# Value tiles of their own in a dilated attention branch, and one tile in place of two for the low halves of the queries

## Chip, cores, metric

One Trainium2 chip, one of its NeuronCores. The metric is device time in microseconds of one execution of the whole program, lower is better. Before the change it is 3742.44 us (median of three runs, 3741.66 to 3744.21).

## What is computed

Two blocks of two layers each, one after the other, over 1024 tokens of width 1024. The change touches the first block only. Each of its layers has three branches on the same normed input; the first and the third are attention:

```python
proj = jnp.einsum('bsd,dc->bsc', h, w_in)
aq, ak, av, az, buv, bz, cq, ck, cv, cz, gl = split_cols(proj)
# first branch: 4 heads, two maps of 64 dims each, causal
qa = partial_rope(aq...); ka = partial_rope(ak...)
oa = diff_attention(qa, ka, va, lam)
# third branch: 8 heads of 64 dims, three dilated windows, their softmaxes merged
qc = partial_rope(cq...); kc = partial_rope(ck...)
oc = sum over patterns of softmax(lse) * dilated_window_attention(qc, kc, vc, window, dil)
yc = oc.reshape(B, S, C_WIDTH) * jax.nn.silu(cz)
pb = jnp.einsum('nbsc,ncd->nbsd', ys, w_branch)
merged = jnp.einsum('bsnd,nbsd->bsd', jax.nn.sigmoid(gl...), pb)
```

The projections `cq`, `ck`, `cv`, `cz` and the gates `gl` all start from the same `h`, so their order is free.

## The kernel before

**Number format.** A float32 value is held as a rounded upper half in fp32r and the remainder as a lower half. A product of two such values takes three TensorE passes (upper by upper, lower by upper, upper by lower). A projection unit is 512 tokens of one block of 128 output columns: 8 contraction blocks by 3 passes, 24 matmuls of 512 columns at L1578, into one PSUM bank. A projection of one name has two such units (tokens 0 to 511, 512 to 1023) on one weight tile. GpSimd makes the two halves of each weight tile (`Whi` at L3001, `Wlo` at L3003) when the tile that stood in that place has been used for the last time; there are three places.

**Order.** Nothing schedules at run time. The class `Order` writes one list of units in Python; each engine's program walks through that list and issues its own part of every unit, in list order, with semaphore waits where a unit needs another's result. `put` and `run` append units. `u["inside"] = {k: [...]}` has TensorE issue another unit's part after contraction block k of u, while the other engines see that unit where it stands in the list.

**Third branch, `attention_c` (L890).** The loop runs over 32 steps: 4 pairs of heads (j), 2 heads (h), 4 groups of 256 queries (i, with 2i+2 key blocks). In step s TensorE issues, in this order: `turn` (transposes of the softmax weights of s at L1705, first into bank `pt`), the scores of s+1 (L1673, L1674), the projection units that the list `amid` gives to this step, and `values` (weights by values, L1721). Behind the scores run, for s+1: VectorE's masked minimum (L2631), ScalarE's exponential (L2042), VectorE's reciprocal (L2673), ScalarE's scaling (L2046). Then come the transposes, ScalarE's upper halves (L2072) and VectorE's lower halves (L2683). The projections in `amid` are what TensorE does meanwhile. Twelve units belong to a pair: two each for values v, the gate z, queries q, keys k, and four for the branch gates g, which are stored to DRAM for later. Before, they are placed so (line 974 to 978): step 0 v0 v1, step 1 z0, step 2 z1, steps 3 to 5 g0 g1 g2, step 6 q0 g3 k0, step 7 q1 k1, where q and k are those of the next pair.

**Queries and keys (`qk`).** VectorE rotates a unit: shuffle L2500, L2504, L2507, L2510, in `tmp0` and `tmp1`. ScalarE writes upper halves (L1983, L1986), VectorE lower halves (L2517 for queries, L2519 for keys). A tile holds two heads in its rows 0 to 63 and 64 to 127 (`ROWS`). `KK[h]` holds head h's keys, upper half in `ROWS[h]` and lower half in the other rows; `QQ[h]` holds the query's upper half twice. So one matmul of 128 contraction rows gives upper by upper plus upper by lower (L1673). A second one (L1674) takes the query's lower halves from `QL[h]`, whose other 64 rows are zero; the unit `clear` (L2590) zeroes them by two VectorE memsets (L2595) at the start of each of the four attention stages.

**Values.** A value unit is projected; ScalarE copies the bank to `tmp0` or `tmp1` (L1994), the same tiles that rotation uses, so the copy waits for the rotation of the units ahead of it; TensorE transposes the copy (unit `v_turn`, L1660) into `pt`; ScalarE and VectorE write halves `VP` (L2007, L2664).

The first branch has the same queries and keys, its own order of units, and 32 steps too.

Of the kernel before, what the change touches and what calls it, by code (L numbers as in the profile page):

```python
# [91 lines left out]
def memory(nc, t):  # L92
# [50 lines left out]
    m.QL = [at(f"QL{i}", o + 4096 * i, [P, S], F32R) for i in range(2)]; o += 8192  # L143
# [3 lines left out]
    m.tmp = [at(f"tmp{i}", o + 2048 * i, [P, 512]) for i in range(4)]; o += 8192  # L147
# [184 lines left out]
class Order:  # L332
# [355 lines left out]
    def attention(self, l, br):  # L688
        diff = br == "a"
        self.tmp_free = [None] * 4  # L690
# [22 lines left out]
        def v_units(j):  # L713
            buf = j % 2
            copied = {}

            def sets(u):
                u["tmp_free"] = listed(self.tmp_free[u.i])
                copied[u.i] = ("v_copied", u.id)

            def turned(u):
                u["copied"], u["rel"] = copied[u.i], v_free[buf:buf + 1] if diff else v_free[:]
                self.tmp_free[u.i] = ("v_turned", u.id)
# [4 lines left out]
            return (self.in1("value", l, COL[br + "v"] + j * P, box={}, sets=sets, emptied="v_copied")  # L728
                    + [Unit(kind="v_turn", i=i, buf=buf, banked=diff, sets=turned, diff=diff, emptied=out if diff else None)
                       for i in range(2)])  # L730
# [21 lines left out]
        cleared = ("cleared", self.put("clear").id)  # L752
# [11 lines left out]
        if not diff:  # L764
            self.banks = NARROW
            self.attention_c(l, qk, vtok, v_free, qk_units, v_units, z_units, gate_units(2), cleared, attended, ztok)
            return
# [14 lines left out]
        def scores(s):  # L782
# [3 lines left out]
                         ready=[x for y in keys for x in y] + [cleared])  # L786
# [103 lines left out]
    def attention_c(self, l, qk, vtok, v_free, qk_units, v_units, z_units, gates, cleared, attended, ztok):  # L890
# [10 lines left out]
        def scores(s, within=False):  # L901
            j, h, i = steps[s]
            keys = [qk["q"][i // 2], qk["k"][0]] + ([qk["k"][1]] if i >= 2 else [])
            scored[s] = self.put("scores", **geometry(s), within=within, ready=[x for y in keys for x in y] + [cleared],
# [54 lines left out]
        self.run([q0, k0, q1])  # L959
# [4 lines left out]
        v = v_units(0)  # L964
        for s, (j, h, i) in enumerate(steps):
            more = s + 1 < len(steps)
            if s % 8 == 0:
# [571 lines left out]
def listed(x):  # L1539
    return x if isinstance(x, list) else [x]  # L1540
# [5 lines left out]
def tensor_program(pe, m, order):  # L1546
# [107 lines left out]
    def v_turn(u):  # L1654
# [4 lines left out]
        for c in range(4):  # L1659
            x = pe.e.transpose(bank[:, c * P:c * P + P], m.tmp[u.i][:, c * P:c * P + P], ident[:, :])  # L1660
        x.then_inc(*pe.tick("v_turned", u.id))

    def scores(u):
        for i, (h, qb) in enumerate(u.maps):
# [5 lines left out]
            for c0 in range(0, nk, 512):  # L1670
# [3 lines left out]
                x = pe.e.matmul(out, m.QL[h][:, qs], m.KK[h][:, c0:c0 + n], start=False, stop=True)  # L1674
# [183 lines left out]
def scalar_program(act, m, order):  # L1858
# [130 lines left out]
    def value(u):  # L1989
# [4 lines left out]
        act.e.activation(m.tmp[u.i][:, :], m.pj[u.bank][:, 0:u.n], ACT.Copy).then_inc(*act.tick("v_copied", u.id))  # L1994
# [304 lines left out]
def vector_program(dve, m, order):  # L2299
# [192 lines left out]
    def qk(u):  # L2492
# [19 lines left out]
        for h, r in enumerate(ROWS):  # L2512
# [3 lines left out]
            if u.name == "q":  # L2516
                TT(m.QL[h][r, c], t1[r, :], m.QQ[h][r, c].bitcast(F32), ALU.subtract).then_inc(*dve.tick("qk_lo", u.id, h))  # L2517
# [454 lines left out]
    parts = {"phase": phase, "start": start, "clear": clear, "square": square, "sums": sums, "last_sums": last_sums, "norm": norm,  # L2972
# [447 lines left out]
```

## Time and profile before

| | us |
|---|---|
| median of three runs | 3742.44 |
| lowest, highest | 3741.66, 3744.21 |
| the profiled execution | 3745.62 |
| its span, from first to last instruction | 3743.6 |
| third branch, first score to last value, layer 1 and 2 | 777.5 to 1149, 2029.6 to 2401 |
| first branch, the same | 363.8 to 666, 1616.1 to 1917 |
| granted TensorE clock, mean | 0.984 |

The profiled execution is 3.18 us over the median. Engines are named PE (TensorE matmul), PEld (its weight loads), DVE (VectorE), ACT (ScalarE), POOL (GpSimd), SP (the queue that issues DMAs). A timeline row gives the start in us, the busy time, engine, line, operation, the tiles written and read, the shape, how many are merged in the row, and in brackets the idle time before it with what ended it. Matmul records overlap, since a matmul's end is its pipeline's end: the pitch of a stream is the distance of two starts.

### The profile page before, as it was taken

The numbers are of one execution on the slowest core, as the hardware profiler recorded it, in microseconds if no ns is written. First come the engines' busy times: TensorE is split into PE (matmuls) and PEld (weight loads), VectorE is DVE, ScalarE is ACT, GpSimd is POOL, SyncE is SP. The second block draws the span as 40 slices with busy tenths as digits, with TensorE's granted clock in tenths as the row PEclk, the third lists the DMA queues.
The fourth block names the chain that finished last, engine by engine and source line by source line (L and its number), as shares of the span: only waits on it lengthen the run. The fifth ranks groups of instructions, "written<-read, shape, count | busy, mean of one in ns | idle before, by whom it ended". The sixth has DMA issues, their size and how long they took to land.

```text
span 3743.6 us, 49479 instructions
## 1 busy us (share of the span) xinstructions
PE 3581.0 (96%) x19870; PEld 3173.4 (85%) x19870; DVE 1873.8 (50%) x3550; ACT 1356.2 (36%) x2965; POOL 1089.9 (29%) x794
## 2 busy tenths in 40 slices
PE   6999999999999999999999999999999999999998
PEld 5888887778887788888877888878999999999998
DVE  5444555356666553155534666655334546424543
ACT  3212444045553121044422555423235532225541
POOL 3632322322222254322322222233530013641111
PEclk9999999999999999999999999999999999999999
DMA  3122111411114311211123111341210012211012
GB/s 108 44 75 71 34 40 40 141 56 46 43 46 157 116 57 51 85 34 40 46 91 105 42 46 46 111 160 48 66 51 21 29 63 89 70 54 33 27 43 91
DMA packets 85476, 244.80 MB, mean 65 GB/s; under 512 B 10752, under 2 KB 24832, under 8 KB 85248
## 3 DMA queue, kind: packets, MB, share of 16 engines
q1 hardware_dynamic: 85248, 241.66, 19.6%
q8 instruction: 156, 2.56, 0.3%
q14 instruction: 72, 0.59, 0.1%
HBM read 191.09 MB, written 50.53 MB: 65 GB/s over the span
## 4 chain that ended last, share of the span: by engine, by line
PE 75%; DVE 12%; ACT 5%; issue 3%; POOL 2%; DMA 1%; SPq 0%; DVEq 0%; POOLq 0%; ACTq 0%
PE pj L1578 28%; PE pS L1578 27%; PE po L1829 4%; PE pS L1809 3%; PE pS L1811 2%; PE po L1721 1%; PE pS L1673 1%; PE pS L1674 1%; DVE tmp L2507 1%; DVE KK L2519 1%; DVE tmp L2510 1%; PE po L1695 1%; PE pj L1821 1%; ACT P L2035 1%; DVE tmp L2500 1%
## 5 line engine op out<-in xcount | busy, mean ns | idle before, releaser
L3001 POOL TENSOR_SCALAR Whi<-stage 128x1024 fp32r<-128x1024 f32 (+3 forms) x252 | 259.5, 1030 | 1833.2 <-PE pj L1578 981.0
L1578 PE MATMUL pj<-Hhi,Whi 128*128 128x512 f32 x1616 | 646.5, 400 | 0.7 <-DVE tmp L2504 0.7
L1578 PE MATMUL pj<-Hhi,Wlo 128*128 128x512 f32 x1616 | 634.7, 393 | 0.0
L1578 PE MATMUL pj<-Hlo,Whi 128*128 128x512 f32 x1616 | 633.0, 392 | 0.0
L3003 POOL TENSOR_TENSOR Wlo<-stage,Whi 128x1024 fp32r<-128x1024 f32 (+3 forms) x252 | 598.5, 2375 | 21.0
L1578 PEld LDWEIGHTS pj<-Hhi,Wlo 128*128 128x128 f32 x1616 | 305.4, 189 | 66.0
L1578 PEld LDWEIGHTS pj<-Hhi,Whi 128*128 128x128 f32 x1616 | 306.6, 190 | 63.9 <-DVE tmp L2504 2.1
L1578 PE MATMUL pS<-Hhi,Whi 128*128 128x512 f32 x816 | 328.1, 402 | 29.4 <-DVE Hlo L2372 13.5
L1578 PEld LDWEIGHTS pj<-Hlo,Whi 128*128 128x128 f32 x1616 | 306.2, 189 | 59.0
L1578 PE MATMUL pS<-Hlo,Whi 128*128 128x512 f32 x816 | 325.0, 398 | 0.0
L1578 PE MATMUL pS<-Hhi,Wlo 128*128 128x512 f32 x816 | 324.4, 398 | 0.0
L1578 PEld LDWEIGHTS pS<-Hhi,Whi 128*128 128x128 f32 x816 | 158.1, 194 | 65.4 <-DVE Hlo L2372 15.2
L2631 DVE CUSTOM_DVE_ANT_0 P<-pS,mask 128x128 f32<-128x128 f32 (+7 forms) x256 | 185.7, 752 | 26.7 <-PE pj L1685 12.0
L1578 PE MATMUL pS<-H2hi,Whi 128*128 128x348 f32 (+1 forms) x576 | 186.8, 324 | 5.1 <-DVE H2lo L2372 3.6
L1578 PEld LDWEIGHTS pS<-Hhi,Wlo 128*128 128x128 f32 x816 | 157.6, 193 | 34.1
L1578 PE MATMUL pS<-H2lo,Whi 128*128 128x348 f32 (+1 forms) x576 | 186.0, 323 | 0.0
L1578 PE MATMUL pS<-H2hi,Wlo 128*128 128x348 f32 (+1 forms) x576 | 185.7, 322 | 0.0
L1578 PEld LDWEIGHTS pS<-Hlo,Whi 128*128 128x128 f32 x816 | 157.7, 193 | 32.6
L2926 DVE TENSOR_REDUCE st<-pS 116x1 f32<-116x1044 f32 (+2 forms) x68 | 84.7, 1245 | 152.1 <-PE pS L1811 151.7
L3049 POOL TENSOR_TENSOR st<-st,vec 128x1 f32<-128x1 f32 x64 | 35.2, 551 | 429.1 <-DVE st L2652 429.1
L1673 PE MATMUL pS<-KK,QQ 128*128 128x512 f32 (+3 forms) x384 | 140.5, 374 | 10.4 <-DVE KK L2519 9.0
L1883 ACT ACTIVATE sq<-X 128x512 f32<-128x512 f32 (+2 forms) x84 | 47.2, 562 | 269.4 <-DVE X L2809 134.7
(485 smaller groups left out, 8013.4 us busy)
## 6 DMA issues: line engine op xcount, KB each, us to landing
stage<-wstream SPq DMA_DIRECT2D x228, 512.0 KB, 3.6
merged<-Mb SPq DMA_DIRECT2D x32, 512.0 KB, 2.8
Mb<-merged SPq DMA_DIRECT2D x32, 512.0 KB, 5.2
gates<-tmp SPq DMA_DIRECT2D x48, 256.0 KB, 2.2
TH<-gates SPq DMA_DIRECT2D x24, 512.0 KB, 6.0
xres<-X SPq DMA_DIRECT2D x16, 520.0 KB, 2.9
xr<-xres SPq DMA_DIRECT2D x16, 520.0 KB, 4.1
X<-xT SPq DMA_DIRECT2D x16, 256.0 KB, 7.1
```

Source lines behind the costliest of these rows:

```text
L1578: x = pe.e.matmul(ps, w[a][:, v.koff + k * P:v.koff + k * P + P], moving(v.of, b, k, v.t0, v.n), start=k == 0 and i == 0, stop=k == v.K - ...
L1673: pe.e.matmul(out, m.QQ[h][:, qs], m.KK[h][:, c0:c0 + n], start=True, stop=False)
L1674: x = pe.e.matmul(out, m.QL[h][:, qs], m.KK[h][:, c0:c0 + n], start=False, stop=True)
L1695: x = pe.e.matmul(m.po[:, 0:P], m.PT[u.pt][:, kb, :], m.V[u.j % 2][:, kb, :], start=kb == 0, stop=kb == u.nb - 1)
L1809: pe.e.matmul(out, q[a][:, qs], m.kn[b][:, t], start=i == 0, stop=False)
L1811: x = pe.e.matmul(out, r[a][:, qs], m.KR[:, t], start=False, stop=a == 1)
L1829: x = pe.e.matmul(m.po[0:u.nq, 0:P], m.PT2[u.l][0:n, i, 0:u.nq], m.V2[u.h][i // 7][0:n, i % 7, :], start=i == 0, stop=i == 8)
L1883: act.e.activation(dst, src, ACT.Square).then_inc(*act.tick("square", u.id))
L2631: dve.e.tensor_tensor_reduce(m.Pm[u.p[i]][:, 0:qb * P + P], m.pS[:, 1024 * i:1024 * i + qb * P + P], m.mask[:, 896 - P * qb:1024], 1.0, 3e ...
L2926: dve.e.tensor_reduce(st[0:u.nq, u.col:u.col + 1], m.pS[0:u.nq, 0:1536].rearrange("p (c n) -> p c n", c=3)[:, :, 0:348], AX.XY, ALU.min).t ...
L3001: pool.e.tensor_scalar(upper, stage, 1.0, 0.0, ALU.mult, ALU.add).then_inc(*pool.tick("whi", c))
L3003: TT(lower, stage, upper.bitcast(F32), ALU.subtract).then_inc(*pool.tick("wlo", c))
```

## The change

1. `QL` is one tile of 128 rows: rows 0 to 63 hold the lower halves of the first head, 64 to 127 those of the second. The second score matmul uses `QL[ROWS[h]]` and `KK[h][ROWS[h]]`, 64 contraction rows. The unit `clear` and every wait for it are gone.
2. In the place of the second `QL` tile stand two tiles `vt0`, `vt1`. In the third branch values are copied there and turned from there; in the first branch they stay in `tmp0`, `tmp1`.
3. In the third branch the values of the next pair are projected in steps 4 and 5, q0 g2 k0 in step 6, q1 g3 k1 in step 7; z0 and z1 in steps 0 and 1, g0 and g1 in 2 and 3. The transposes of the values stand inside z0 and z1, after contraction block 1. In the last pair, which has no next one, steps 4 and 7 have no projection (before: step 7 alone). At the branch's start the order is q0 v0 k0 v1 q1 k1 in place of q0 k0 q1 k1 and then, in step 0, v0 v1.

```diff
-    m.QL = [at(f"QL{i}", o + 4096 * i, [P, S], F32R) for i in range(2)]; o += 8192
+    m.QL = at("QL", o, [P, S], F32R); o += 4096
+    own = [at(f"vt{i}", o + 2048 * i, [P, 512]) for i in range(2)]; o += 4096
...
-    m.tmp = [at(f"tmp{i}", o + 2048 * i, [P, 512]) for i in range(4)]; o += 8192
+    m.tmp = [at(f"tmp{i}", o + 2048 * i, [P, 512]) for i in range(4)] + own; o += 8192
...
         def v_units(j):
-            buf = j % 2
+            buf, t = j % 2, 0 if diff else 4
...
-                u["tmp_free"] = listed(self.tmp_free[u.i])
+                u["tmp_free"] = listed(self.tmp_free[t + u.i])
...
-        cleared = ("cleared", self.put("clear").id)
...
-        self.run([q0, k0, q1])
+        v = v_units(0)
+        self.run([q0, v[0], k0, v[1], q1])
         k1["inside"] = {4: [scores(0, True)]}
...
-                v[1]["inside"], z[0]["inside"] = {5: v[2:3]}, {3: v[3:4]}
-                amid = [v[0:1] + v[2:3] + v[1:2], v[3:4] + z[0:1], z[1:2], g[0:1], g[1:2], g[2:3], g[3:4], []]
+                z[0]["inside"], z[1]["inside"] = {1: v[2:3]}, {1: v[3:4]}
+                amid = [v[2:3] + z[0:1], v[3:4] + z[1:2], g[0:1], g[1:2], [], g[2:3], g[3:4], []]
                 if j < 3:
                     read, v = [], v_units(j + 1)
                     q, k = qk_units(j + 1, {(x, i): read for x in "qk" for i in range(2)})
-                    amid[6], amid[7] = [q[0], g[3], k[0]], k[1:2]
+                    amid[4:] = [v[0:1], v[1:2], [q[0], g[2], k[0]], [g[3], k[1]]]
...
-            x = pe.e.transpose(bank[:, c * P:c * P + P], m.tmp[u.i][:, c * P:c * P + P], ident[:, :])
+            x = pe.e.transpose(bank[:, c * P:c * P + P], m.tmp[u.t + u.i][:, c * P:c * P + P], ident[:, :])
...
-                x = pe.e.matmul(out, m.QL[h][:, qs], m.KK[h][:, c0:c0 + n], start=False, stop=True)
+                x = pe.e.matmul(out, m.QL[ROWS[h], qs], m.KK[h][ROWS[h], c0:c0 + n], start=False, stop=True)
...
-                TT(m.QL[h][r, c], t1[r, :], m.QQ[h][r, c].bitcast(F32), ALU.subtract).then_inc(*dve.tick("qk_lo", u.id, h))
+                TT(m.QL[r, c], t1[r, :], m.QQ[h][r, c].bitcast(F32), ALU.subtract).then_inc(*dve.tick("qk_lo", u.id, h))
...
-    def clear(u):
-
-        for x in u.ph:
-            dve.wait_ge(x)
-        for h in range(2):
-            dve.e.memset(m.QL[h][ROWS[1 - h], :].bitcast(F32), 0.0).then_inc(*dve.tick("cleared", u.id, h))
-        dve.mark("cleared", u.id)
```

What moves is seen best on ScalarE where one pair gives way to the next (`PC` weights turned, `P` weights, `VP` values turned; L2072 upper halves of the turned weights). Before:

```order
L1983 ACTIVATE KK_84<-tmp_93 64x512
L1983 ACTIVATE KK_85<-tmp_93 64x512
L2072 ACTIVATE PC_101<-pt 128x128
L2072 ACTIVATE PC_101<-pt 128x2x128
L2081 ACTIVATE tmp_95<-po 64x256
...
L1870 ACTIVATE Yhi<-tmp_95 64x512
L1994 ACTIVATE tmp_92<-pj 128x512
L2007 ACTIVATE VP_90<-pt 128x4x64
L2007 ACTIVATE VP_91<-pt 128x4x64
L1994 ACTIVATE tmp_93<-pj 128x512
```

and now:

```order
L1959 ACTIVATE tmp_95<-pj 128x512
L1983 ACTIVATE KK_84<-tmp_94 64x512
L1983 ACTIVATE KK_85<-tmp_94 64x512
L2072 ACTIVATE PC_102<-pt 128x128
L2072 ACTIVATE PC_102<-pt 128x2x128
L2081 ACTIVATE tmp_96<-po 64x256
...
L1870 ACTIVATE Yhi<-tmp_96 64x512
L2007 ACTIVATE VP_91<-pt 128x4x64
L2007 ACTIVATE VP_92<-pt 128x4x64
L1965 ACTIVATE tmp_95<-pj 128x512
```

The copies of the value units (L1994) have left this place for steps 4 and 5 of the pair before, and a gate (L1959) stands ahead of the last key unit.

On TensorE the fifth step of the last pair (first layer), which reads before, up to its first two projection matmuls:

```order
L1705 MATMUL pt<-ident,P_96 128x128
L1705 MATMUL pt<-ident,P_97 128x128 x2
L1673 MATMUL pS<-KK_85,QQ_83 128x384
L1674 MATMUL pS<-KK_85,QL_87 128x384
L1673 MATMUL pS<-KK_85,QQ_83 128x512
L1674 MATMUL pS<-KK_85,QL_87 128x512
L1578 MATMUL pj<-Hhi,Whi_62 128x512
L1578 MATMUL pj<-Hlo,Whi_62 128x512
```

now reads, into the sixth:

```order
L1705 MATMUL pt<-ident,P_97 128x128
L1705 MATMUL pt<-ident,P_98 128x128 x2
L1673 MATMUL pS<-KK_85,QQ_83 128x384
L1674 MATMUL pS<-KK_85,QL 128x384
L1673 MATMUL pS<-KK_85,QQ_83 128x512
L1674 MATMUL pS<-KK_85,QL 128x512
L1721 MATMUL po<-PC_102,VP_92 128x256
L1721 MATMUL po<-PC_104,VP_92 128x256
L1721 MATMUL po<-PC_102,VP_92 128x128
L1721 MATMUL po<-PC_104,VP_92 128x128
L1705 MATMUL pt<-ident,P_97 128x128 x3
L1705 MATMUL pj<-ident,P_98 128x128 x4
```

The 24 projection matmuls between the scores and the values of this step are gone. The order of the score matmuls, one of `QQ` and one of `QL` in turn, is as it was.

## Rows read from the trace of the kernel before

**Rows 1.** The page: busy time, and engines in the chain that ended last

```profile
PE 3581.0 (96%) x19870; PEld 3173.4 (85%) x19870; DVE 1873.8 (50%) x3550; ACT 1356.2 (36%) x2965; POOL 1089.9 (29%) x794
...
PE 75%; DVE 12%; ACT 5%; issue 3%; POOL 2%; DMA 1%; SPq 0%; DVEq 0%; POOLq 0%; ACTq 0%
```

**Rows 2.** PE waits over the whole span: us in total, times, longest

```profile
PE pt L1660 <- ACT tmp L1994: 15.8, 6, 2.6
...
PE pt L1705 <- ACT P L2046: 9.6, 2, 6.2
PE pS L1673 <- DVE KK L2519: 9.0, 8, 2.0
```

**Rows 3.** Groups of tile QL: duration ns min/median/max, first and last start

```profile
L1674 PE MATMUL pS<-KK,QL x384: 272/387/628, 364.0 to 2388.2; 128*128 128x512 f32 x136, 128*128 128x128 f32 x24, 128*128 128x384 f32 x24, 128*128 128x256 f32 x8
...
L2595 DVE MEMSET QL<- x8: 912/912/912, 333.8 to 2016.1; 64x1024 f32 x8
```

**Rows 4.** PE timeline round a 16-row matmul: start us, us busy, instruction, [idle before]

```profile
2542.91 0.40 PE L1578 MATMUL pj<-Hlo,Whi 128*128 128x512 f32 x1
2543.14 0.39 PE L1578 MATMUL pj<-Hhi,Wlo 128*128 128x512 f32 x1
2543.46 1.25 PE L1614 MATMUL pS<-ident,st 16*128 16x16 f32 x8
2544.47 0.48 PE L1578 MATMUL pj<-Hhi,Whi 128*128 128x512 f32 x1
```

**Rows 5.** PE timeline, the same line L1614 with 128 rows throughout

```profile
2563.17 1.05 PE L1614 MATMUL pj<-ident,st 128*128 128x128 f32 x8
2564.05 0.39 PE L1614 MATMUL pS<-ident,st 128*128 128x128 f32 x2
2564.20 0.40 PE L1578 MATMUL pS<-H2hi,Whi 128*128 128x348 f32 x1
```

**Rows 6.** Timeline of PE where pair 0 of heads gives way to pair 1

```profile
879.42 0.40 PE L1578 MATMUL pj<-Hhi,Wlo 128*128 128x512 f32 x1
...
882.67 0.39 PE L1578 MATMUL pj<-Hhi,Whi 128*128 128x512 f32 x1
...
891.96 0.39 PE L1578 MATMUL pj<-Hhi,Wlo 128*128 128x512 f32 x1
894.98 0.65 PE L1660 MATMUL pt<-ident,tmp 128*128 128x128 f32 x4 [2.63 <-ACT tmp L1994]
...
897.26 0.65 PE L1721 MATMUL po<-PC,VP 128*128 128x256 f32 x4 [0.24 <-DVE VP L2664]
```

**Rows 7.** Timeline of DVE, the same stretch

```profile
875.99 2.63 DVE L2507 TENSOR_TENSOR tmp<-tmp,sin 128x512 f32<-128x512 f32 x1
...
884.41 0.74 DVE L2500 STREAM_SHUFFLE tmp<-pj 128x512 f32<-128x512 f32 x1
...
887.96 1.40 DVE L2519 TENSOR_TENSOR KK<-tmp,KK 64x512 fp32r<-64x512 f32 x2 [0.70 <-ACT KK L1983]
889.39 0.62 DVE L2683 TENSOR_TENSOR PC<-pt,PC 128x128 fp32r<-128x128 f32 x2
```

**Rows 8.** Timeline of POOL, the same stretch

```profile
875.67 2.39 POOL L3003 TENSOR_TENSOR Wlo<-stage,Whi 128x1024 fp32r<-128x1024 f32 x1
```

**Rows 9.** Timeline of ACT, the same stretch

```profile
892.44 1.21 ACT L2046 ACTIVATE P<-P,st 128x384 f32<-128x384 f32 x2
...
895.67 0.66 ACT L2007 ACTIVATE VP<-pt 128x256 fp32r<-128x256 f32 x2 [0.74 <-PE pt L1660]
```

**Rows 10.** PE timeline, first transposes of a fifth step (here of the last pair)

```profile
1117.33 0.51 PE L1705 MATMUL pt<-ident,P 128*128 128x128 f32 x3
```

**Rows 11.** ACT timeline, the weights of the step after it

```profile
1121.25 1.22 ACT L2046 ACTIVATE P<-P,st 128x384 f32<-128x384 f32 x2
```

**Rows 12.** Timeline of PE at the start of the third branch, first layer

```profile
786.46 1.14 PE L1705 MATMUL pt<-ident,P 128*128 128x128 f32 x3 [6.19 <-ACT P L2046]
```

**Rows 13.** Timeline of DVE where the first branch starts its softmax

```profile
364.29 0.29 DVE L2631 CUSTOM_DVE_ANT_0 P<-pS,mask 128x128 f32<-128x128 f32 x1 [3.01 <-PE pS L1674]
```

More of the change, by code:

```diff
@@ L689, in attention @@
         diff = br == "a"
-        self.tmp_free = [None] * 4
+        self.tmp_free = [None] * 6
         qk = {"q": [None] * 2, "k": [None] * 2}
@@ L722, in turned @@
                 u["copied"], u["rel"] = copied[u.i], v_free[buf:buf + 1] if diff else v_free[:]
-                self.tmp_free[u.i] = ("v_turned", u.id)
+                self.tmp_free[t + u.i] = ("v_turned", u.id)
                 vtok[buf][u.i] = (out, u.id)
@@ L727, in v_units @@
             out = "v_out" if diff else "v_low"
-            return (self.in1("value", l, COL[br + "v"] + j * P, box={}, sets=sets, emptied="v_copied")
-                    + [Unit(kind="v_turn", i=i, buf=buf, banked=diff, sets=turned, diff=diff, emptied=out if diff else None)
+            return (self.in1("value", l, COL[br + "v"] + j * P, box={}, sets=sets, t=t, emptied="v_copied")
+                    + [Unit(kind="v_turn", i=i, t=t, buf=buf, banked=diff, sets=turned, diff=diff, emptied=out if diff else None)
                        for i in range(2)])
@@ L765, in attention @@
             self.banks = NARROW
-            self.attention_c(l, qk, vtok, v_free, qk_units, v_units, z_units, gate_units(2), cleared, attended, ztok)
+            self.attention_c(l, qk, vtok, v_free, qk_units, v_units, z_units, gate_units(2), attended, ztok)
             return
@@ L785, in scores @@
             u = self.put("scores", **geometry(s), free=[("masked", softened[s - 1].id, m) if s else None for m in (0, 0, 1, 1)],
-                         ready=[x for y in keys for x in y] + [cleared])
+                         ready=[x for y in keys for x in y])
             scored[s] = u
@@ L888, in attention, with attention_c @@
         attended(softened[s], scored[s])
-    def attention_c(self, l, qk, vtok, v_free, qk_units, v_units, z_units, gates, cleared, attended, ztok):
+    def attention_c(self, l, qk, vtok, v_free, qk_units, v_units, z_units, gates, attended, ztok):
         steps = [(j, h, i) for j in range(4) for h in range(2) for i in range(4)]
@@ L903, in scores @@
             keys = [qk["q"][i // 2], qk["k"][0]] + ([qk["k"][1]] if i >= 2 else [])
-            scored[s] = self.put("scores", **geometry(s), within=within, ready=[x for y in keys for x in y] + [cleared],
+            scored[s] = self.put("scores", **geometry(s), within=within, ready=[x for y in keys for x in y],
                                  free=[("masked", softened[s - 1].id, m) if s else None for m in (0, 0, 1, 1)])
@@ L963, in attention_c @@
         self.run([k1])
-        v = v_units(0)
         for s, (j, h, i) in enumerate(steps):
@@ L1993, in value @@
         phase_met(u)
-        act.e.activation(m.tmp[u.i][:, :], m.pj[u.bank][:, 0:u.n], ACT.Copy).then_inc(*act.tick("v_copied", u.id))
+        act.e.activation(m.tmp[u.t + u.i][:, :], m.pj[u.bank][:, 0:u.n], ACT.Copy).then_inc(*act.tick("v_copied", u.id))
     def v_turn(u):
@@ L2970, in last @@
                 op1=ALU.mult).then_inc(*dve.tick("final2", u.c, k))
-    parts = {"phase": phase, "start": start, "clear": clear, "square": square, "sums": sums, "last_sums": last_sums, "norm": norm,
+    parts = {"phase": phase, "start": start, "square": square, "sums": sums, "last_sums": last_sums, "norm": norm,
              "table": table, "proj": proj,
```

## The prediction

> **What bounds the kernel.** I read the page first: which engine is busy, and which one the chain that ended last runs along. TensorE is busy for 96% of the span and makes 75% of the chain [rows 1]. So a wait is worth what it holds TensorE up, and an instruction of another engine is worth nothing by itself. Then I read what TensorE waits for [rows 2]. In the third branch three causes stand out: six waits for the copy of the values (15.8 us), two for the first softmax weights (9.6 us), eight for key halves (9.0 us, some 4 of them at the two starts of this branch, by the timeline). The change aims at these. Last I read what else it touches in TensorE's stream: 384 matmuls of `QL`, each between two others of 128 rows [rows 3]. They become matmuls of 64 rows. A faster or slower form of them lies on the path in full. A difference of 0.2%, 7.5 us, is about what a measurement of this kernel tells from none.
>
> **1. The 64-row matmuls.** No row shows a 64-row matmul. The trace has one place where a matmul uses fewer row groups of the array than its neighbours: L1614 with 16 rows, after and before matmuls of 128. An ordinary pitch of 512 columns is 2543.14 - 2542.91 = 0.23 us; to the 16-row matmul it is 0.32 [rows 4]. In the control, the same line with 128 rows, eight starts take 2564.05 - 2563.17 = 0.88 us, 0.11 each, and the last two take 0.15 up to the next fp32r matmul, 0.07 less than 0.22 [rows 5]. So from 2543.14 to the first L1578 behind it, one pitch of 0.23 and eight of 0.11 less 0.07, 1.04 us, would be expected; it took 2544.47 - 2543.14 = 1.33 [rows 4]. One way into the narrow form and one way out cost 0.29 us, though the narrow matmuls stream 16 columns and not 128. I take 0.29 us for each of the 384, since this is the nearest row by far: 111 us. Bounds: below, nothing (64 rows may be treated otherwise than 16; a gain is excluded, as the columns streamed stay the same and no two 64-row matmuls are neighbours). Above, each matmul waits for the whole of the one before (0.39 us) and for a weight load of 0.19 that is no longer hidden, in place of a 0.23 pitch: 0.35 for each of 768 changes, 269 us. None of this is covered: scores lie between transposes and projections of a busy engine.
>
> The Trainium skill, page "TensorE: Matmul & The Clock Gate", section "Why this matters for your kernels", states that a single small-K matmul takes the same time as one with K=128. By it the 111 us would be zero; that is a rival below. The page "TensorEngine Tiling (Array Packing)", section "Tiling Modes", says that a change of the tiling mode drains the engine, without a figure; the 0.29 us agree.
>
> **2. Where one pair gives way to the next, six times.** Now the transposes of the values wait 894.98 - 891.96 - 0.23 = 2.8 us for the copy, and the first values 0.4 us more for `VP` [rows 6]: 3.2 us. After the change the copy is made long before, and the transposes stand 6 matmuls into z0. What is late next is bank `pt`: VectorE has to take the lower halves of the turned weights from it (L2683), and that is queued behind the last key unit. Count from the last projection matmul of k1 (879.42). TensorE needs 882.67 - 879.42 = 3.25 us to the next projection [rows 6], 0.6 more for two pairs of scores by term 1, and 6 pitches of 0.23: it arrives at 5.2. VectorE starts k1's rotation at 0.5 (the gate now ahead of k1 lets it be idle by then) and needs 887.96 + 1.40 - 884.41 = 4.95 when nothing disturbs it [rows 7]. But the weight split follows each last use of a weight tile, and while POOL's L3003 runs [rows 8] VectorE's L2507 takes 2.63 us in place of 0.68 [rows 7], 1.95 more. I assume the same for k1, whose end frees a weight tile. So its keys are ready at 7.4, and `pt` at 7.4 + 0.65 (889.36 to 890.01) = 8.05: a wait of 2.85. Then 4 transposes, 0.5, and 18 matmuls, 4.1, bring TensorE to values at 12.7. `VP` needs the softmax chain of the next step, which ends 893.65 - 889.36 = 4.3 after the keys [rows 7, 9], a conversion of Y, which I put at 0.65, and from `VP`'s start to the values 897.26 - 895.67 = 1.6 [rows 6, 9]: 7.4 + 6.55 = 13.95, a wait of 1.25. Together 4.1 against 3.2: +0.9, six times, **+5 us**. The wait doesn't go, it changes its cause. Bounds: -19 if both waits vanish; +20 if VectorE's unit ends as late as now (9.9 after the matmul, 2.5 more).
>
> **3. The last pair.** Its fifth step loses its cover. From its transposes, 1117.33 [rows 10], to the first weights of the step after, 1121.25 + 0.61 [rows 11], are 4.5 us. TensorE has 0.3 of transposes, 0.9 + 0.6 of scores and 0.45 of values to do. That leaves 2.3, and 0.3 more for the second map's weights: 2.6 us in each layer, **+5**. Bounds 0 to +8.
>
> **4. The branch's start.** Now the first transposes wait 6.2 us in layer 1 [rows 12], 3.4 in layer 2 (9.6 in all [rows 2]), and scores about 2 each time. Behind the change the scores stand 11 us of values later than k0 and don't wait, but the last two units, q1 and k1, still follow each other, and the softmax is queued on VectorE behind q1 with a weight split beside it. With term 2's times for a rotation I get some 3.8 us for the weights and 2.3 for `pt`, 6.1 against 9.7 and 6.8 with the small gaps: **-4** for both. Bounds -13 to 0.
>
> **5. The memsets.** Eight of 0.91 us [rows 3], on VectorE. In the first branch the softmax starts after an idle time of 3.0 us of VectorE, in wait for scores [rows 13]: nothing. In the third they are in term 4.
>
> **6. The rest** costs nothing: ScalarE's copies are the same number and ScalarE is 36% busy; POOL splits as many tiles; SP's gate DMAs only change places. If TensorE's longer steps give covers elsewhere, that is below 0.3 us a step.
>
> **Sum.** 111 + 5 + 5 - 4 = +117 us. The profiled execution took 3745.62, 3.2 over the median; so 3742.4 + 117 = **3859 us**, 3.1% slower.
>
> **Rivals.**
> - *No price for 64 rows.* For it: the narrow row in the trace is one case, of 16 rows and of another number format. Against it: the way out of the narrow form has no semaphore wait in it, and it is slow there too. Without the longer scores term 2 is 1.5 each, +9, term 3 is +6, term 4 about -2: 3742.4 + 13 = 3755 us, still slower. This is the case of the skill's small-K rule. 0.14.
> - *Faster.* 64 rows cost nothing, and the keys are ready before TensorE gets to the transposes. The point from which it decides: k1's lower halves must end within 4 us of k1's last matmul, not 7.4; it would need POOL's split to fall elsewhere and a shorter rotation. Then -19 in term 2, -4 in term 4, +5 in term 3: 3724 us. Against it stands the undisturbed 4.95. 0.05.
> - *Full exposure.* The bound above of term 1: 3742.4 + 269 + 6 = 4017 us. The odd row gives half of it. 0.04.
> - The change not doing what it says is term 2 itself: the tiles are free, another wait takes the place. It is in every case but the second.
>
> **Numbers.** The forecast has 0.77. Its own range takes term 1 between 0.15 and 0.36 us for each matmul (one way of 0.09 in and as much less out; both ways at the narrow row's worst) and the other terms' nearer bounds: 3790 to 3900. To leave out no more than 2 in 10 I reach down a little, to 3785. Slower by over 0.2%: forecast, full exposure and nine tenths of the first rival, 0.93, cut to 0.91 for what I haven't thought of. Within: 0.03. Faster: 0.06.
>
> **What would show it.** In the profile after: the start of a `QL` matmul 0.09 us or more later behind its `QQ` neighbour than the 0.23 pitch of 512 columns, weight loads of scores no longer beside the matmul before, and the scores' stretch longer by 0.29 for each pair. Six waits of L1660 now put down to VectorE's L2683 in place of ScalarE's copy, of 2 to 4 us; waits of L1721 for `VP` of about 1 us; two waits of L1705 of some 2.5 us in the last pairs. No memset L2595. I am wrong if the pitch of `QL` matmuls stays 0.23, and wrong on term 2 if L1660 has no wait in the third branch.

## The result, and the profile after

| | before | after |
|---|---|---|
| median, us | 3743.32 (4 runs, 3741.66 to 3748.87) | 3886.32 (4 runs, 3877.61 to 3896.09) |
| profiled execution, its span | 3745.62, 3743.6 | 3884.86, 3883.1 |
| granted TensorE clock, mean | 0.984 | 0.979 |
| start of the first to start of the last `QQ` score matmul, first branch, layers 1 and 2 | 288.2, 287.4 | 315.5, 311.1 |
| the same, third branch | 357.9, 358.4 | 392.9, 392.7 |

The changed kernel is slower, by a ratio of 1.038 (95% interval 1.0353 to 1.0407). The forecast was 3859, 3.1% slower, with a range of 3785 to 3900. So the direction held, and the loss was 143 us where 117 were forecast. The spans of the two profiled executions differ by 139.5 us; the accounts below are made against that.

The page of the profile after: busy time, chain, and the groups of the two score matmuls (columns: line, engine, operation, count | busy us, mean ns | idle before).

```profile
PE 3731.9 (96%) x19870; PEld 3202.5 (82%) x19870; DVE 1866.8 (48%) x3542; ACT 1357.1 (35%) x2965; POOL 1089.5 (28%) x794
...
PE 86%; DVE 6%; ACT 2%; issue 2%; DMA 1%; POOL 1%; SPq 0%; DVEq 0%; POOLq 0%; ACTq 0%
...
L1674 PE MATMUL pS<-KK,QL 64*128 64x512 f32 (+3 forms) x384 | 171.5, 447 | 0.0
L1673 PE MATMUL pS<-KK,QQ 128*128 128x512 f32 (+3 forms) x384 | 169.7, 442 | 0.9 <-ACT V L2004 0.9
```

TensorE made 75% of the chain before [rows 1] and makes 86% now. It has the same 19870 instructions and is busy for 3731.9 us where it was for 3581.0: the same work got longer. The median `QL` matmul lasts 491 ns where it lasted 387 [rows 3], and its `QQ` neighbour 474 where it lasted 390.

What TensorE waits for, after (us in total, times, longest):

```profile
PE pt L1660 <- DVE PC L2675: 19.0, 6, 3.3
PE pt L1705 <- ACT P L2046: 13.4, 4, 5.0
...
PE pt L1728 <- ACT PT L2054: 7.3, 13, 0.8
PE pt L1685 <- DVE st L2644: 5.9, 2, 2.9
...
PE po L1721 <- DVE VP L2656: 2.2, 2, 1.1
```

Against [rows 2]: the copy of the values has gone as a cause, and the same six transposes wait longer, for bank `pt`. The waits for key halves (9.0 us) are gone. L1728, the transposes of the first branch's results, waited 15.2 us before, in 19 places.

**The scores.** I call a matmul of 128 rows wide and one of 64 rows narrow, and each step from one to the other, either way, a change of form. TensorE after, where wide and narrow matmuls of 512 columns stand in turn, and its weight loads there:

```profile
503.86 0.48 PE L1673 MATMUL pS<-KK,QQ 128*128 128x512 f32 x1
504.27 0.49 PE L1674 MATMUL pS<-KK,QL 64*128 64x512 f32 x1
504.69 0.50 PE L1673 MATMUL pS<-KK,QQ 128*128 128x512 f32 x1
505.12 0.49 PE L1674 MATMUL pS<-KK,QL 64*128 64x512 f32 x1
505.54 0.50 PE L1673 MATMUL pS<-KK,QQ 128*128 128x512 f32 x1
```

```profile
504.27 0.18 PEld L1674 LDWEIGHTS pS<-KK,QL 64*128 64x128 f32 x1 [0.24 <-issue]
504.69 0.19 PEld L1673 LDWEIGHTS pS<-KK,QQ 128*128 128x128 f32 x1 [0.24 <-issue]
```

The pitch is 0.41 to 0.43 us, where 512 columns took 0.23 from a `QL` matmul to the next. In the kernel before, at such a place, TensorE's matmuls and then its weight loads:

```profile
470.70 0.39 PE L1674 MATMUL pS<-KK,QL 128*128 128x512 f32 x1
470.93 0.22 PE L1673 MATMUL pS<-KK,QQ 128*128 128x128 f32 x1
```

```profile
470.47 0.19 PEld L1674 LDWEIGHTS pS<-KK,QL 128*128 128x128 f32 x1
470.70 0.19 PEld L1673 LDWEIGHTS pS<-KK,QQ 128*128 128x128 f32 x1
```

Before, a weight load starts one matmul early (the load at 470.47 is for the matmul at 470.70) and is hidden by it. After, it starts with its own matmul (504.27 and 504.27), in both directions, and its 0.18 to 0.19 us lie bare. The medians of the pitches say the same at other widths. From a `QL` matmul to what follows: 0.23 to 0.43 us at 512 columns, 0.18 to 0.37 at 384, 0.12 to 0.31 at 256, 0.11 to 0.25 at 128: some 0.19, whatever the columns, 0.14 for the narrowest. From `QQ` to `QL` it is 0.28 to 0.43 us at 512 columns, 0.15 more, and 0.19 more at the other widths. I weight the shift of each median with its count (of `QQ` to `QL` and of `QL` to the next): 137 us for 384 matmuls, 0.36 each, 0.18 for each of 768 changes of form.

What follows the scores pays a little too. After, where a projection stands behind them:

```profile
906.74 0.50 PE L1578 MATMUL pj<-Hhi,Whi 128*128 128x512 f32 x1
907.07 0.40 PE L1578 MATMUL pj<-Hlo,Whi 128*128 128x512 f32 x1
907.31 0.40 PE L1578 MATMUL pj<-Hhi,Wlo 128*128 128x512 f32 x1
```

The first pitch of the projection, at full clock, is 0.34 us where the kernel before has 0.23 behind its scores. With some 60 such places that is 6 us, on top of the 137. With 128 rows in the new order (experiment 1) it is 0.23 again.

### The profile page after: what moved, and what is told of

Same layout as the page of the kernel before. It is cut to its first block, busy times and chain, and to the rows that moved or that the text cites. A ratio compares the mean times of both kernels' runs of the same rounds, so it can differ in the third digit from the quotient of the medians.

```text
span 3883.1 us, 49441 instructions
## 1 busy us (share of the span) xinstructions
PE 3731.9 (96%) x19870; PEld 3202.5 (82%) x19870; DVE 1866.8 (48%) x3542; ACT 1357.1 (35%) x2965; POOL 1089.5 (28%) x794
## 4 chain that ended last, share of the span: by engine, by line
PE 86%; DVE 6%; ACT 2%; issue 2%; DMA 1%; POOL 1%; SPq 0%; DVEq 0%; POOLq 0%; ACTq 0%
PE pj L1578 35%; PE pS L1578 27%; PE po L1829 4%; PE pS L1674 3%; PE pS L1673 3%; PE pS L1809 3%; PE pS L1811 2%; PE po L1721 2%; PE po L1695 1%; PE pj L1821 1%; PE pt L1685 1%; DMA TH<-gates 1%; PE pj L1705 1%; PE pt L1705 1%; DVE tmp L2510 1%
## 5 line engine op out<-in xcount | busy, mean ns | idle before, releaser
L1578 PE MATMUL pj<-Hhi,Whi 128*128 128x512 f32 x1616 | 658.3, 407 | 0.0
L2995 POOL TENSOR_TENSOR Wlo<-stage,Whi 128x1024 fp32r<-128x1024 f32 (+3 forms) x252 | 598.7, 2376 | 21.0
L1674 PE MATMUL pS<-KK,QL 64*128 64x512 f32 (+3 forms) x384 | 171.5, 447 | 0.0
L1673 PE MATMUL pS<-KK,QQ 128*128 128x512 f32 (+3 forms) x384 | 169.7, 442 | 0.9 <-ACT V L2004 0.9
```

The source lines that it names most:

```text
L1578: x = pe.e.matmul(ps, w[a][:, v.koff + k * P:v.koff + k * P + P], moving(v.of, b, k, v.t0, v.n), start=k == 0 and i == 0, stop=k == v.K - ...
L1673: pe.e.matmul(out, m.QQ[h][:, qs], m.KK[h][:, c0:c0 + n], start=True, stop=False)
L1674: x = pe.e.matmul(out, m.QL[ROWS[h], qs], m.KK[h][ROWS[h], c0:c0 + n], start=False, stop=True)
L2995: TT(lower, stage, upper.bitcast(F32), ALU.subtract).then_inc(*pool.tick("wlo", c))
```

## The experiments

**1 and 2: the narrow form and the rest of the change apart.** The first takes the changed kernel and gives the second score matmul its 128 rows back. The second puts only the 64-row matmul into the kernel before.

```diff
-                x = pe.e.matmul(out, m.QL[ROWS[h], qs], m.KK[h][ROWS[h], c0:c0 + n], start=False, stop=True)
+                x = pe.e.matmul(out, m.QL[:, qs], m.KK[h][:, c0:c0 + n], start=False, stop=True)
```

> The changed kernel with one edit: the second score matmul takes all 128 rows of QL and KK again. With one QL tile the other 64 rows now add the other head's lower halves times this head's lower key halves, a product of two remainders, of the size of those that the scheme drops anyway. So the new order, the value tiles and the missing memsets stay, the 64-row form goes. Forecast's theory (the 64-row form is nearly all of the loss): back near the kernel before, 3742 + 13 = 3755 us by the sum's terms without term 1; by the waits in the profile after (pt +3, VP +1, first weights +4, keys -9) only 3742 to 3748. Rival, the new order and its waits cost the most and the form little: 3800 us or more. Pitch of QL matmuls of 512 columns: 0.23 to 0.28 us by the first, 0.43 by the second.

Measured: 3760.27 us, ratio 1.0042 (1.0029 to 1.0055), 14.6 us above the kernel before. The forecast's theory holds: nearly all of the loss has gone with the narrow form. What is left is nearer its sum (+13) than the 3742 to 3748 that the waits in the profile after would give, because without the longer scores these waits are longer, L1660's 21.3 us in place of 19.0, and L1728 has its own back. Score matmuls stand in turn here as they do in the kernel after, on the same tiles and into the same banks, so neither the turns nor the banks make the price.

```diff
-                x = pe.e.matmul(out, m.QL[h][:, qs], m.KK[h][:, c0:c0 + n], start=False, stop=True)
+                x = pe.e.matmul(out, m.QL[h][ROWS[h], qs], m.KK[h][ROWS[h], c0:c0 + n], start=False, stop=True)
```

> The kernel before with one edit: the second score matmul takes 64 rows (both QL tiles, the memsets and the old order stay). Forecast's theory: 384 of them at 0.29 us, 3742 + 111 = 3853 us. Theory from the profile after, 768 changes of form at 0.195 us, 150 us, less 8 to 10 of waits that the longer scores cover: 3880 to 3885. Rival, the order costs the most: below 3800.

Measured: 3843.44 us, ratio 1.0274 (1.0253 to 1.0296): +98 us, less than either theory said. The pitches are those of the kernel after to 2 ns (430, 427), so the price of 137 us is the same. The rest was given back, as the waits of this kernel show:

```profile
PE pt L1728 <- ACT PT L2054: 7.2, 13, 0.8
...
PE pS L1673 <- DVE KK L2519: 3.9, 2, 1.9
...
PE pt L1705 <- ACT P L2046: 2.2, 2, 1.1
```

L1660's 15.8 us of [rows 2] have no row any more, L1705 has 2.2 of 9.6, L1673 3.9 of 9.0, L1728 7.2 of 15.2. 137 - 15.8 - 7.4 - 5.1 - 8.0 = 101. So TensorE's longer scores covered 36 us of waits in the old order. With the 6 us behind the scores the sum is 107, against 98 measured (95 between the spans): the account is good to 10 us. In the new order this cover is much smaller: 3886.32 - 3760.27 = 126 us is what the narrow form costs there.

**3 and 4: price by matmul or by change of form.** The same 384 narrow matmuls, regrouped. In 3 the `QQ` matmuls of a map come first, then its `QL` ones (512 changes of form). In 4 this is done over both maps of a unit (256 changes).

```diff
-            for c0 in range(0, nk, 512):
-                n = min(512, nk - c0)
+            tiles = [(c0, min(512, nk - c0)) for c0 in range(0, nk, 512)]
+            for c0, n in tiles:
                 out = m.pS[:, 1024 * i + c0:1024 * i + c0 + n]
                 pe.e.matmul(out, m.QQ[h][:, qs], m.KK[h][:, c0:c0 + n], start=True, stop=False)
+            for c0, n in tiles:
+                out = m.pS[:, 1024 * i + c0:1024 * i + c0 + n]
                 x = pe.e.matmul(out, m.QL[ROWS[h], qs], m.KK[h][ROWS[h], c0:c0 + n], start=False, stop=True)
```

> The changed kernel with the score matmuls of a map regrouped: first the QQ matmuls of its one or two banks, then the QL ones. The same 384 matmuls of 64 rows, but 512 changes of form in place of 768. If each change costs 0.195 us: 3886 - 50 = 3836 us. If each 64-row matmul costs 0.35 us by itself, whatever stands beside it: 3886. If the cost is the switch of the accumulating bank or the reuse of loaded weights, something else: no move, or a gain at maps of one bank too (it leaves those as they are).

> The changed kernel with the score matmuls of a whole unit regrouped: QQ matmuls of both maps, then the QL ones of both: 256 changes of form. If each change costs 0.195 us: 3886 - 100 = 3786 us, less some us given back where the second map's bank comes free late; in the first branch the 64-row matmuls of the two maps stand in different row groups and may even overlap, a few us more. If each 64-row matmul costs by itself: 3886 or above.

Measured: 3834.48 us (ratio 1.0238, 1.0224 to 1.0252) and 3784.59 us (1.0109, 1.0094 to 1.0124): 52 and 102 us below the changed kernel, where 50 and 100 were expected by change of form and none by matmul. From the start of the first to the start of the last `QQ` score matmul, mean of both layers:

| changes of form in one branch | 0 (experiment 1) | 64 (4) | 128 (3) | 192 (after) |
|---|---|---|---|---|
| third branch, us | 357.7 | 371.4 | 381.2 | 392.8 |
| first branch, us | 289.3 | 290.1 | 301.9 | 313.3 |

In the third branch this is nearly a straight line, 35.1 / 192 = 0.18 us for each change. In the first branch the steps from 64 to 128 and to 192 are as steep (11.8 and 11.4 us), and the one from 0 to 64 is 0.8 us. There the narrow matmuls of the two maps read different rows. TensorE of experiment 4, in the first branch and then in the third (rows of L1676 are the four `QL` matmuls of a unit):

```profile
487.22 1.05 PE L1672 MATMUL pS<-KK,QQ 128*128 128x512 f32 x4
488.21 0.69 PE L1676 MATMUL pS<-KK,QL 64*128 64x512 f32 x4
488.82 0.66 PE L1688 MATMUL pt<-ident,P 128*128 128x128 f32 x4
...
1119.05 1.12 PE L1672 MATMUL pS<-KK,QQ 128*128 128x512 f32 x4
1120.10 1.14 PE L1676 MATMUL pS<-KK,QL 64*128 64x512 f32 x4
1121.17 0.50 PE L1578 MATMUL pj<-Hhi,Whi 128*128 128x512 f32 x1
```

Four of 512 columns take 488.82 - 488.21 = 0.61 us in the first branch and 1121.17 - 1120.10 = 1.07 in the third, where both maps belong to one head. In the first branch the two heads' matmuls start 2 to 12 ns apart: rows 0 to 63 and 64 to 127 work side by side. What that saves (0.46 us for four of 512 columns) about pays for the two changes of form (0.36), and no more.

**5: the value tiles without the new order.** Everything of the changed kernel but its order, with 128-row matmuls.

```diff
-        v = v_units(0)
-        self.run([q0, v[0], k0, v[1], q1])
+        self.run([q0, k0, q1])
...
-                amid = [v[2:3] + z[0:1], v[3:4] + z[1:2], g[0:1], g[1:2], [], g[2:3], g[3:4], []]
+                amid = [v[0:1] + v[2:3] + v[1:2], v[3:4] + z[0:1], z[1:2], g[0:1], g[1:2], g[2:3], g[3:4], []]
...
-                    amid[4:] = [v[0:1], v[1:2], [q[0], g[2], k[0]], [g[3], k[1]]]
+                    amid[6], amid[7] = [q[0], g[3], k[0]], k[1:2]
```

> The order of the kernel before, with everything else of the changed kernel: value tiles of their own, one QL tile, no memsets, and the second score matmul on 128 rows. It tells what the tiles are worth without the new order. If the copy of the values really waits for tmp0 and tmp1, its six waits (15.8 us) and a little at the start go: 3745 - 12 = 3733 us or less. Rival, from ScalarE's timeline of the kernel before: there the copy L1994 starts at 894.33, right behind the scaling L2046 and the copy L1870 that end at 894.31, so it waits in ScalarE's queue and the tile was free since 887.3: no change, 3741 to 3748 us, and L1660 still waits 2.6 us.

Measured: 3744.16 us, ratio 0.9999 (0.9991 to 1.0008), no change. ScalarE of this kernel, and the transposes that wait for it, at one place and in all:

```profile
888.79 0.63 ACT L1870 ACTIVATE Yhi<-tmp 64x512 fp32r<-64x512 f32 x1
889.45 0.60 ACT L1994 ACTIVATE vt<-pj 128x512 f32<-128x512 f32 x1
```

```profile
890.10 0.66 PE L1660 MATMUL pt<-ident,vt 128*128 128x128 f32 x4 [2.63 <-ACT vt L1994]
```

```profile
PE pt L1660 <- ACT vt L1994: 15.8, 6, 2.6
```

The copy now has a tile of its own and still starts right behind L1870, 2.63 us late as before [rows 6], and the six waits sum to the same 15.8 us [rows 2]. It waited in ScalarE's queue, behind the softmax, and not for the tile. The memsets are gone here too and moved nothing.

**6: what makes `pt` late.** The boundary of two pairs in the kernel after, first TensorE, then VectorE, then POOL:

```profile
919.58 0.40 PE L1578 MATMUL pj<-Hhi,Wlo 128*128 128x512 f32 x1
...
924.76 0.40 PE L1578 MATMUL pj<-Hhi,Wlo 128*128 128x512 f32 x1
928.24 0.66 PE L1660 MATMUL pt<-ident,vt 128*128 128x128 f32 x4 [3.09 <-DVE PC L2675]
...
932.64 0.39 PE L1578 MATMUL pj<-Hhi,Wlo 128*128 128x512 f32 x1
934.13 0.65 PE L1721 MATMUL po<-PC,VP 128*128 128x256 f32 x4 [1.11 <-DVE VP L2656]
```

```profile
921.43 1.21 DVE L2507 TENSOR_TENSOR tmp<-tmp,sin 128x512 f32<-128x512 f32 x1
922.75 2.69 DVE L2510 SCALAR_TENSOR_TENSOR tmp<-tmp,tmp 128x512 f32<-128x512 f32 x1
926.13 1.40 DVE L2519 TENSOR_TENSOR KK<-tmp,KK 64x512 fp32r<-64x512 f32 x2 [0.69 <-ACT KK L1983]
927.57 0.62 DVE L2675 TENSOR_TENSOR PC<-pt,PC 128x128 fp32r<-128x128 f32 x2
```

```profile
922.19 2.70 POOL L2995 TENSOR_TENSOR Wlo<-stage,Whi 128x1024 fp32r<-128x1024 f32 x1
```

The whole of k1's rotation stands in VectorE's queue ahead of the lower halves that free `pt`. Counted by pitches the two waits of TensorE are 3.25 and 1.26 us, 4.5 together, each some 0.15 over its bracket. The next kernel takes experiment 1, moves k1 into the first step of the next pair, behind that pair's first softmax, and starts the branch otherwise.

```diff
-        self.run([q0, v[0], k0, v[1], q1])
-        k1["inside"] = {4: [scores(0, True)]}
+        self.run([q0, v[0], k0, v[1]])
+        q1["inside"] = {1: [scores(0, True)]}
...
-        self.run([k1])
+        self.run([q1])
+        late = k1
...
-                z[0]["inside"], z[1]["inside"] = {1: v[2:3]}, {1: v[3:4]}
-                amid = [v[2:3] + z[0:1], v[3:4] + z[1:2], g[0:1], g[1:2], [], g[2:3], g[3:4], []]
+                late["inside"], z[1]["inside"] = {1: v[2:3]}, {1: v[3:4]}
+                amid = [v[2:3] + [late], v[3:4] + z[1:2], g[0:1], g[1:2], [], g[2:3], g[3:4], []]
...
-                    amid[4:] = [v[0:1], v[1:2], [q[0], g[2], k[0]], [g[3], k[1]]]
+                    amid[4:] = [v[0:1], v[1:2], [q[0], g[2], k[0]], [g[3]]]
+                    late = k[1]
...
+                self.run(z[0:1] if s % 8 == 1 else [])
                 scores(s + 1)
```

> e1 (new order, 128 rows) with the last key unit k1 moved out of the pair's last step into the first step of the next pair, in the place of z0, and z0 in front of the second step's scores, z1 behind them. The branch starts with q0 v0 k0 v1, then the first scores inside q1, and k1 in step 0. Theory: the 4.5 us that TensorE loses where pairs change (transposes behind bank pt 3.3, values behind VP 1.1) come from k1's rotation of 5 us, which stands in VectorE's queue ahead of the lower halves of the turned weights and of the next softmax. Behind them it holds nothing up, since scores need these keys only in the step after: 3760 - 6 x 4.5 - 2 x 5 at the starts = 3723 us, and less half clock, 3715 to 3730. Rival: the rotation now holds up the weights of the second step, and the scores behind z0 wait for the keys: the waits come back there, 3745 to 3765.

Measured: 3745.03 us, ratio 1.0003 (0.9995 to 1.0012), 15 us below experiment 1 where 37 were expected. TensorE at the start of the branch, and at the first change of pairs:

```profile
789.50 1.11 PE L1663 MATMUL pt<-ident,vt 128*128 128x128 f32 x4 [7.10 <-DVE PC L2678]
...
886.26 0.66 PE L1663 MATMUL pt<-ident,vt 128*128 128x128 f32 x4 [0.89 <-DVE PC L2678]
...
892.15 0.65 PE L1724 MATMUL po<-PC,VP 128*128 128x256 f32 x4 [1.14 <-DVE VP L2659]
```

Where pairs change the theory holds in direction: by pitches 2.3 us in place of 4.5. They don't go, since now q1's rotation stands there, and it takes 9.7 us (875.9 to 885.6), with POOL splitting weights beside it twice. At the start a wait of 7.1 us has come up, behind the same q1.

**7: `pt` alone.** Experiment 1 with the transposes in a projection bank (`banked=True`).

> e1 with the transposes of the third branch's values in a projection bank, not in pt. If the 3.3 us of L1660 in wait for pt are a cause by themselves: 3760 - 20 = 3740 us. If pt is only the first of several things that k1's rotation makes late, the wait moves to the values (VP, whose copies stand in ScalarE's queue behind the next scaling): L1660 has none, L1721 waits 3 to 4.5 us at each of the six places, time 3755 to 3760.

Measured: 3768.74 us, ratio 1.0077 (1.0064 to 1.0091). The waits of this kernel:

```profile
PE po L1719 <- DVE VP L2654: 31.6, 8, 5.5
```

The transposes (L1660 above) wait no more, and the values wait, by pitches, 4.9 to 5.7 us at each of six places. In experiment 1 the two waits together were 3.6 to 4.8. This is the second theory, but 9 us above its 3755 to 3760. The bank was a link in the chain, not its cause.

**8 to 11: following the chain.** 9 is experiment 6 with the start in the order q0 k0 v0 q1 v1, the first transposes of the values inside q1. 8 has them there too, in the old start order, and moves the later ones; 10 is 9 with q1 also put behind the change of pairs; 11 is 10 with another bank for half of the second step's turned weights. Experiment 9 against experiment 6:

```diff
-        self.run([q0, v[0], k0, v[1]])
-        q1["inside"] = {1: [scores(0, True)]}
+        self.run([q0, k0, v[0]])
+        v[2]["within"] = True
+        q1["inside"] = {1: [scores(0, True)], 3: v[2:3]}
...
-        self.run([q1])
+        self.run([v[2], q1, v[1]])
...
-                late["inside"], z[1]["inside"] = {1: v[2:3]}, {1: v[3:4]}
-                amid = [v[2:3] + [late], v[3:4] + z[1:2], g[0:1], g[1:2], [], g[2:3], g[3:4], []]
+                late["inside"], z[1]["inside"] = {1: v[2:3]} if j else None, {1: v[3:4]}
+                amid = [(v[2:3] if j else []) + [late], v[3:4] + z[1:2], g[0:1], g[1:2], [], g[2:3], g[3:4], []]
```

> e6 with the first transposes of the values moved. At the branch's start they stand in q1 after contraction block 3, ahead of the first softmax weights' turn, since pt is free there; in e6 they waited 7.1 us for pt in each layer, behind q1's rotation. At the six places where pairs change they stand after block 3 of k1 in place of block 1, and ScalarE and VectorE take VP ahead of the output copy (L1873) of the pair before. Theory, from the waits of e6: 14.2 us at the two starts go, and of 2.3 us at the six places 0.65 each: 3745 - 14 - 4 = 3727 us, half clock behind the long waits a few us less. Rival: at the start VP's lower halves now hold up q1's rotation or the turn of the first weights, or the key rotations behind them wait: 3735 to 3745 us.

> e6 with another start of the third branch and nothing else: q0 k0 v0, then q1 with the first scores behind block 1 and the first transposes of the values behind block 3, then v1, then k1 in step 0. In e6 TensorE lost 7.3 us there in each layer, in wait for pt behind q1's rotation (9 us, two of its operations stretched beside POOL's splits). With v1 between q1 and the first weights the rotation has 5.5 us more: 3745 - 2 x 6 = 3733 us. Rival: the half-stretched rotation still comes out late at the first values or the second weights, 3738 to 3745.

> e9 with q1 as well behind the change of pairs: step 7 has only g3 (scores inside it), step 0 q1, step 1 k1 and z0, scores, z1. At the six places no rotation then stands ahead of the turned weights' lower halves: the wait of 1.05 us for pt goes, the one for VP (1.3) may stay or halve: e9 - 6 x 1.5 = 3724 us. Rival, as e8 showed it: with two banks a projection now starts right behind the one whose bank VectorE has not read yet, and waits 1 to 3.6 us there, six times: e9 + 5 to + 15.

> e10 with one edit: in the pair's second step the second half of the turned weights goes to the second score bank of map 0, which the short scores of this step leave free, in place of a projection bank. In e10 z0 waits 3.2 to 4.0 us there, six times, since VectorE reads that bank behind q1's rotation. If this bank was the cause: 3759 - 22 = 3737 us, and with the waits at the places where pairs change at 0.6 us in place of e9's 2.35, half clock less too, down to 3726. Rival: z1 now waits for the bank that k1's rotation reads, or the scores for the new bank: 3745 or more.

| | us | ratio (interval) | the wait that came up in TensorE |
|---|---|---|---|
| 8 | 3765.24 | 1.0051 (1.0038 to 1.0065) | z0 for the bank that k1's rotation reads, 6 times; values at each start, 3.2 us |
| 9 | 3735.72 | 0.9974 (0.9963 to 0.9985) | none of this size |
| 10 | 3759.49 | 1.0036 (1.0024 to 1.0048) | z0 for a bank behind q1's rotation, 6 times |
| 11 | 3761.79 | 1.0048 (1.0035 to 1.0062) | second step's scores for k1's keys; scores for the new bank once in each layer, 3.5 us |

Their rows in the lists of waits, of 8, 10 and 11:

```profile
PE pj L1584 <- DVE tmp L2510: 20.6, 6, 3.4
```

```profile
PE pj L1582 <- DVE PC L2679: 22.0, 6, 3.8
```

```profile
PE pS L1682 <- DVE KK L2528: 27.1, 14, 3.5
```

8, 10 and 11 are misses: 3727, 3724 and 3737 us were expected. The rivals foresaw that another wait would come up, but for 8 and 10 not how much: 3735 to 3745 and 3741 to 3751 were their ranges, 3765 and 3759 came. Each experiment removes the wait it aims at, and another of 3 to 4 us comes up. I read this as two rotations of 5 to 10 us on VectorE that must pass somewhere in this stretch; no run takes one of them away to show it. Part of the size is the clock: the traces have 139 us at half clock in 8 and 145 in 10, against 121 in 6 and 118 in 9, and in 8 the stretch 890.8 to 897.5, behind a wait of 3.4 us of z0, is one of them. Only at the start was there room. **Experiment 9 beats both kernels**, the one before by 0.26% and the one after by 151 us. Its 9 us below experiment 6 are 3 short of what was expected: scores now wait for k1's keys, up to 2.0 us, in the place of the 7.1. Its own rows:

```profile
PE pS L1677 <- DVE KK L2523: 10.1, 10, 2.0
...
PE pt L1664 <- DVE PC L2679: 5.4, 6, 0.9
```

## Why the prediction was right, and where it was off

- **Term 1, the 64-row matmuls (+111).** The cause was right and the size too small: 0.36 us for each matmul, 137 us, not 0.29 and 111, so 26 us short, and 6 more behind the scores. The narrow row that I took it from [rows 4] is one matmul of 16 rows. The step that failed outright is "none of this is covered": longer scores hid waits that ended on other engines. Between before and after, L1728 lost 7.9 us, the key halves 9.0 and L1685 1.5. Some 4 of the 9.0 had gone by the order alone (experiment 1 has 4.9 left), so the cover is about 14 us. That the total still came within 26 us of the forecast is in part luck: price too low and cover left out go against each other. The upper bound of 0.35 for each change was a wait for the whole of the matmul before plus a bare load; what the runs show is 0.18 for each, no more than the bare load of 0.18 to 0.19.
- **Term 2, six changes of pairs (+5).** Right in kind and size. From k1's last matmul, at 919.58, TensorE came to the transposes at 5.4 us (said: 5.2), `pt` was free at 8.6 (8.05), values started at 14.55 (13.95). The waits were 3.25 and 1.26 us (2.85 and 1.25); at the later changes of pairs only the first exists, 3.2 to 3.5. The split on POOL beside a rotation step was assumed, and is there: 2.69 us at 922.75. Sum by the rows: 19.0 + 2.2 - 15.8 - 1.5 = +4 us.
- **Term 3, the last pair (+5).** Right. Rows of its fifth step, in the kernel after:

```profile
1181.97 0.67 PE L1721 MATMUL po<-PC,VP 128*128 128x256 f32 x4 [0.22 <-DVE tmp L2684]
1184.40 0.55 PE L1705 MATMUL pt<-ident,P 128*128 128x128 f32 x3 [1.76 <-ACT P L2046]
```

The two steps of TensorE that wait are 0.49 and 1.97 us longer than unhindered by pitches, 2.46 in each layer (said: 2.6). Some 0.2 of the 0.49 is the bare load behind a narrow matmul, which term 1 has already.

- **Term 4, the starts (-4).** The first weights wait 4.95 us in both layers, where I had 3.8; the 2.3 us for `pt` did not come. With the small gaps that is 10.2 in place of 9.7 + 6.8, -6 us.
- **Term 5, the memsets (0)** and the copies in **term 6**: right, by experiment 5.
- **No term: the clock.** The granted clock fell from 0.984 to 0.979. Here is the step behind term 3's wait, after; and then the matching stretch before (columns: stretch, its length, TensorE busy us and instructions, clock, DMA share, GB/s):

```profile
1186.20:1192.80 6.60, 6.60 (x15) 0.50 0.00 0
```

```profile
1117.50:1127.00 9.50, 9.50 (x52) 1.00 0.31 96
```

TensorE is busy throughout and at 1.2 GHz, half of 2.4; just before, it had sat idle 1.76 us behind the narrow scores, and before the change it had had projections there. Two more stretches at half clock, 1035.9 to 1039.3 and 1141.7 to 1145.1, lie right behind waits of L1660 of 3.4 to 3.5 us; the one at 928.24, of 3.25, has none behind it. Over the whole trace TensorE had half clock for 166 us after and 122 before. With the new order alone (experiment 1) it is 142, with the narrow form alone (experiment 2) 118. So the narrow form by itself takes nothing from the clock; the new order does, and both together most. The clocks of the single executions say the same: 0.981 to 0.985 in experiment 2, 0.979 to 0.981 in experiment 1, 0.977 to 0.981 after, and 0.982 to 0.985 for the kernel before beside experiments 1 and 2. Why the form takes more in the new order was not separated.

The account of the spans: +137 for the form; waits +3.2 (L1660), +3.8 (L1705), +0.7 (`VP`), -9.0 (keys), -7.9 (L1728), -1.5 (L1685); that makes +126. Some 13 of the 139.5 are left. The projections' pitches took 14.6 us more: 6 in the first one behind the scores, and the rest, 8, mostly at half clock.

**The rivals.** *No price for 64 rows* put the time at 3755. Experiment 1 is this case built for real, 3760: its premise was wrong, and its schedule terms (+13 forecast, +14.6 measured) fit in sum better than in parts. By the rows of the two lists of waits the changes of pairs gave +6 where it had +9, and all its terms together about +9; the rest lies outside them, 2 us of it in slower projections. The Trainium skill, page "TensorE: Matmul & The Clock Gate", section "Why this matters for your kernels", gives a small-K matmul the time of one with K=128. Between narrow neighbours the runs agree: in experiment 4 four of one head took 1.07 us, 0.27 each, about as long as the four wide ones before them (1.05). Between wide neighbours they don't: 0.43 in place of 0.23. *Full exposure* had 0.35 for each change; half was right.

The page "TensorEngine Tiling (Array Packing)", section "Key Properties", says that a change of the tiling mode drains the engine and that different tiles can load and multiply in parallel. The second shows here, in the two heads' matmuls side by side (0.61 against 1.07 us). Of the first the runs show the bare load, 0.18 us at each change (experiments 3 and 4); a wait for the whole of the matmul before does not show, since the record at 503.86 lasts 0.48 us and the next one starts at 504.27, as far as modelled ends can tell.

That the tiles would be free and another wait take the place was said of all cases but *Faster*, and held further than I took it: even in the kernel before, the tile was never what the copy waited for (experiment 5), though the first part of the prediction counts those 15.8 us as what the change aims at.

## What to carry to other kernels

A matmul of 64 rows saved nothing here and, set between wide ones, cost its own weight load and the next one's; leave the rows full and let them add something harmless (here a product of two remainders), or put the narrow ones side by side. Before giving a buffer of its own to an instruction that seems to wait for one, look in its engine's timeline whether it starts right behind its predecessor: then it is queued, and only the order helps. A price on a busy engine is paid less what it hides, so test the parts of a change apart: here the same narrow form cost 98 us in one order and 126 in the other.

## What the runs showed that I had not expected

- At a change of form the cost hardly depends on the columns: on the way out about 0.19 us at 256, 384 and 512, with the weight load starting together with its matmul. The first projection pitch behind it is 0.11 us longer as well.
- The narrow form alone did not lower the granted clock (118 us at half clock against 122); the new order did (142).
- Narrow matmuls of the two row halves into different banks start 2 to 12 ns apart and run side by side.
- Steps of VectorE's rotation that read two tiles stretched from 0.7 us to 2.6 or 2.7 beside POOL's L2995 (2.69 us at 922.75); one rotation met two splits and took 9.7 us in place of 5 (experiment 6).
